# A hybrid two-block layer on one core: experts in pairs on the two column halves of TensorE, in plain full precision, with longer rings for their weights

## The reference

```python
def hier_moe(h, w_group, b_group, w_expert, b_expert, w_gate_e, w_up_e, w_down_e):
    ...
    g_top, g_idx = lax.top_k(g_prob, 1)
    ...
    e_top, e_idx = lax.top_k(e_prob, TOP_K)
    w = g_top * e_top / jnp.sum(e_top, axis=-1, keepdims=True)
    ...
    for e in range(N_EXPERTS):
        a = jax.nn.silu(h @ w_gate_e[e]) * (h @ w_up_e[e])
        y = y + gates[:, e:e + 1] * (a @ w_down_e[e])
    return y
```

## Time and profile before

| what | us |
|---|---|
| median of three runs | 2104.88 |
| fastest run | 2102.53 |
| slowest run | 2868.25 |
| span of the profiled execution | 2102.3 |

### The profile page before, as it was taken

The page is one execution under the profiler, slowest core; times in us unless marked ns, Lnnn a source line. Parts: engine busy times, 40 slices in busy tenths (PEclk is TensorE's granted clock), DMA queues, the critical chain, the costliest instruction groups (busy, mean ns, idle before and its releaser), DMA issues. The chain is left out here.

```text
span 2102.3 us, 25437 instructions
## 1 busy us (share of the span) xinstructions
PE 1936.8 (92%) x8950; PEld 1391.0 (66%) x8954; DVE 1116.4 (53%) x1765; ACT 756.8 (36%) x1230; POOL 234.0 (11%) x285
## 2 busy tenths in 40 slices
PE   4997995799999689999999999998999999999997
PEld 2445644566666356676788887874667678888785
DVE  3787734687878568765222222345976622222235
ACT  2034421355555232672233332222277213333222
POOL 1000000233323134001000000003500100000001
PEclk9999997899999899999999999999999999999998
DMA  9162013599997620022033342331002213335131
GB/s 378 64 240 83 24 58 120 189 362 366 356 353 280 245 81 1 22 91 80 21 100 96 89 154 70 114 119 74 1 22 91 61 32 92 96 100 160 60 100 41
DMA packets 148058, 267.18 MB, mean 127 GB/s; under 512 B 11456, under 2 KB 108736, under 8 KB 134784
## 3 DMA queue, kind: packets, MB, share of 16 engines
q1 hardware_dynamic: 141776, 256.29, 34.5%
q0 software_dynamic: 6192, 9.70, 1.4%
HBM read 257.57 MB, written 20.97 MB: 132 GB/s over the span
## 5 line engine op out<-in xcount | busy, mean ns | idle before, releaser
L274 PE MATMUL bank<-ht_hi,gate_up_hi 128*128 128x512 f32 x704 | 274.2, 389 | 3.4 <-ACT arena L1441 3.4
L276 PE MATMUL bank<-ht_hi,gate_up_lo 128*128 128x512 f32 x704 | 274.0, 389 | 0.0
L275 PE MATMUL bank<-ht_lo,gate_up_hi 128*128 128x512 f32 x704 | 274.0, 389 | 0.0
L2412 PE MATMUL bank<-arena 128*128 128x512 f32 (+3 forms) x640 | 196.4, 466 | 8.0 <-ACT arena L1288 5.5
L1769 DVE TENSOR_TENSOR expert_gate_up_lo<-expert_gate_up,expert_gate_up_hi 128x2048 fp32r<-128x2048 f32 x64 | 146.6, 2292 | 58.0 <-ACT expert_gate_up_hi L1204 58.0
L2066 DVE TENSOR_TENSOR arena<-arena,bank 128x512 f32 (+1 forms) x44 | 30.3, 688 | 272.6 <-ACT arena L1307 272.6
L2412 PEld LDWEIGHTS bank<-arena 128*128 128x128 f32 x640 | 114.7, 196 | 84.4 <-issue 67.0
L274 PEld LDWEIGHTS bank<-ht_hi,gate_up_hi 128*128 128x128 f32 x704 | 132.2, 188 | 31.5 <-issue 4.2
L275 PEld LDWEIGHTS bank<-ht_lo,gate_up_hi 128*128 128x128 f32 x704 | 132.2, 188 | 27.6
L276 PEld LDWEIGHTS bank<-ht_hi,gate_up_lo 128*128 128x128 f32 x704 | 132.2, 188 | 27.3
L1204 ACT CAST expert_gate_up_hi<-expert_gate_up 128x2048 fp32r<-128x2048 f32 x64 | 121.6, 1901 | 72.0 <-PE bank L276 71.9
(11 more groups left out here) (359 smaller groups left out, 3510.2 us busy)
## 6 DMA issues: line engine op xcount, KB each, us to landing
gate_up_whole<-w_gu SPq DMA_DIRECT2D x88, 512.0 KB, 5.0
expert_gate_up<-w_gate_e SPq DMA_DIRECT2D x32, 1024.0 KB, 7.1
expert_gate_up<-w_up_e SPq DMA_DIRECT2D x32, 1024.0 KB, 9.8
arena<-w_down_e SPq DMA_DIRECT2D x32, 1024.0 KB, 5.2
down_whole<-w_down SPq DMA_DIRECT2D x44, 512.0 KB, 3.5
arena<-w_ada SPq DMA_DIRECT2D x5, 4096.0 KB, 20.5
arena<-w_in SPq DMA_DIRECT2D x4, 2048.0 KB, 15.9
w_o_whole<-w_o SPq DMA_DIRECT2D x2, 4096.0 KB, 13.5
```

The costliest lines, as they stand in the source:

```text
L274: pe.matmul(ps, xh, wh, start=start, stop=False)
L275: pe.matmul(ps, xh, wl, start=False, stop=False)
L276: return pe.matmul(ps, xl, wh, start=False, stop=stop)
L2412: ins = pe.matmul(ps[:, 0:b - a], HT[:, c, t * P:(t + 1) * P], w_in2[j][:, c], start=c == 0, stop=c == C8 - 1)
```

## The change

Experts are taken in pairs. The left 64 columns of PE's array hold the first 64 rows of the even expert's window, the right 64 columns those of the odd one. For each of the 8 feature blocks one matmul goes to each half, with that expert's own gate and up weights moving, and both write the same bank, one to partitions 0 to 63, the other to 64 to 127. All is done on the float32 values as they are loaded, with no high and low parts, so ACT and DVE have no splitting. PE's list is no longer staggered: gate and up of a pair, its transposes, its down matmuls, then the next pair. The loops over experts are written out.

Rows beyond an expert's first 64 are taken in windows of 128 after the last pair, one window at a time, in a loop that runs at least once (`extras`). For each such window the expert's three matrices are loaded once more and the whole array is used. DVE works out which expert and which column each of them has.

The ring for gate and up has five slots, the one for down four. Loads: experts 0 and 1 complete, with the router's weights ahead of them, once the attention's output is turned; gate and up of 2 and 3 after the last mixing matmuls, their down tiles after the token rows; gate and up of expert 4 when all sorted rows are in `XsT`. Then in turn, per pair p: when its gate and up matmuls have ended, gate and up of experts 2p+5 and 2p+6; when its down matmuls have ended, down of 2p+4 and 2p+5. The slot lists for storing have 32 columns (16 pairs, up to 16 extra windows) in place of 128. The tiles move within the same arena to make room.

```diff
-        ring_hi = [part(f"expert_gate_up_hi{n}", base + 4 * GU + 2 * DN + n * (GU // 2), 2, C8 // 2, FE) for n in range(2)]
-        stage = [at(base + 3 * GU, T, D), H]
+        ring = [*(at(base + n * GU, 2, C8, FE) for n in range(4)), at(H0 + 2 * D, 2, C8, FE)]
+        ring_d = [at(base + 4 * GU + n * DN, 2, D) for n in range(DN_RING)]
```

SP:

```diff
-            with sp.Fori(1, NE // 4) as it:
-                for s in range(4):
-                    refill(it * 4 + s, it * 4 + s, it * 4 + s - 2, s)
+            load_gate_up(4, gu_slot(4))
+            for p in range(EPAIRS - 2):
+                sp.wait_ge(m_gu, p + 1)
+                for e in (2 * p + 5, 2 * p + 6):
+                    if e < NE:
+                        load_gate_up(e, gu_slot(e))
+                sp.wait_ge(m_y, p + 1)
+                for e in (2 * p + 4, 2 * p + 5):
+                    load_down(e, dn_slot(e))
...
+            with sp.Fori(0, extras) as x:
+                e = sp.value_load(extra_i[0:1, 0, bass.ds(x, 1)], min_val=0, max_val=NE - 1)
+                sp.wait_ge(m_gfree, x + 1)
+                load_gate_up(e, gu_slot(NE))
+                sp.wait_ge(m_dfree, x + 1)
+                load_down(e, dn_slot(NE))
```

ACT:

```diff
-                act.copy(ring_hi[half], ring[s][:, :, 4 * half:4 * half + 4]).then_inc(m_whi, 1)
+            def silu(p, b):
+                act.wait_ge(m_gu, p + 1)
+                act.activation(SG[:, b], bank[b][:, 0:FE], ACT.Silu).then_inc(m_silu, 1)
```

DVE:

```diff
-                dve.tensor_tensor(ring_lo[s][:, :, c4], ring[s][:, :, c4], ring_hi[half].bitcast(F32), ALU.subtract).then_inc(m_wlo, 1)
+            def window(p):
+                for h in range(2):
+                    w0 = dve.value_load(win[0:1, 2 * p + h:2 * p + h + 1], min_val=0, max_val=2 * S)
+                    ins = dve.tensor_copy(XW[p % 2][:, :, HALF * h:HALF * h + HALF], XsT[:, :, bass.ds(w0, HALF)])
+                ins.then_inc(m_xw, 1)
...
+            for p in range(EPAIRS):
...
+                product(p, b)
+                if p + 2 < EPAIRS:
+                    dve.wait_ge(m_gu, p + 1)
+                    window(p + 2)
...
+                copy_ya(p, b)
+            extras = dve.value_load(n_extra[0:1, 0:1], min_val=1, max_val=EXTRAS)
+            with dve.Fori(0, extras) as x:
+                w0 = dve.value_load(extra_i[0:1, 1, bass.ds(x, 1)], min_val=0, max_val=2 * S)
+                dve.wait_ge(m_gu, x + EPAIRS)
+                dve.tensor_copy(XW[0], XsT[:, :, bass.ds(w0, P)]).then_inc(m_xw, 1)
...
```

PE:

```diff
-            with pe.Fori(0, last) as g:
-                for s in range(3):
-                    gate_up(g * 4 + s + 1, g, s + 1)
-                    down(g * 4 + s, g, s)
-                    turn_a(g * 4 + s + 1, s + 1)
+            for p in range(EPAIRS):
...
+                for e in (2 * p, 2 * p + 1):
+                    pe.wait_ge(s_gu[gu_slot(e)], 32 * (e // len(GU_SLOT) + 1))
+                for c in range(C8):
+                    for h in range(2):
+                        ins = pe.matmul(bank[b][half_rows(h)], XW[b][:, c, half_rows(h)], ring[gu_slot(2 * p + h)][:, :, c], start=c == 0, stop=c == C8 - 1)
+                ins.then_inc(m_gu, 1)
...
+                turn_a(p, b)
+                pe.wait_ge(m_atc, p + 1)
...
+                for e in (2 * p, 2 * p + 1):
+                    pe.wait_ge(s_dn[dn_slot(e)], 16 * (e // DN_RING + 1))
+                for half in range(2):
+                    for c in range(2):
+                        for h in range(2):
+                            ins = pe.matmul(bank[4 + 2 * b + half][half_rows(h)], AT[:, b, c, half_rows(h)],
+                                            ring_d[dn_slot(2 * p + h)][:, c, 512 * half:512 * half + 512], start=c == 0, stop=c == 1)
+                ins.then_inc(m_y, 1)
```

More of the change, by code:

```diff
@@ L1239, in _ @@
-            copy_at(0, 0)
-            def step(n, g, s, ahead):
-                g2, s2 = (g, s + 2) if s < 2 else (g + 1, s - 2)
-                if ahead:
-                    gate_up_high(n + 2, g2, s2, 0)
-                silu(n + 1, (s + 1) % 4)
-                if ahead:
-                    gate_up_high(n + 2, g2, s2, 1)
-                copy_y(n, g, s)
-                copy_at(n + 1, (s + 1) % 4)
-            with act.Fori(0, last) as g:
-                for s in range(4):
-                    step(g * 4 + s, g, s, True)
@@ L1257, in weight_second @@
+            with act.Fori(0, extras) as x:
+                act.wait_ge(m_a, x + EPAIRS)
+                silu(x + EPAIRS, 0)
+                act.wait_ge(m_y, x + EPAIRS)
+                copy_at(x + EPAIRS, 0)
+                act.wait_ge(m_st[0], 16 * (EPAIRS // 2 + x))
+                copy_y(x + EPAIRS, 0)
             def weight_second(t):
@@ new lines, in product, with copy_ya @@
+            def product(p, b):
+                dve.wait_ge(m_silu, p + 1)
+                dve.tensor_tensor(A[:, b], SG[:, b], bank[b][:, FE:], ALU.mult).then_inc(m_a, 1)
+            def copy_ya(p, b):
+                dve.wait_ge(m_y, p + 1)
+                dve.tensor_copy(Y[:, b, 0:512], bank[4 + 2 * b][:]).then_inc(m_ya, 1)
+            own.settle()
+            window(0)
+            window(1)
+            for p in range(EPAIRS):
+                b = p % 2
+                if p >= 2:
+                    dve.wait_ge(m_at, p - 1)
+                product(p, b)
+                if p + 2 < EPAIRS:
+                    dve.wait_ge(m_gu, p + 1)
+                    window(p + 2)
+                if p >= 2:
+                    dve.wait_ge(m_st[b], 16 * (p // 2))
+                copy_ya(p, b)
@@ L2382, in _ @@
-            for s in range(3):
-                gate_up(last * 4 + s + 1, last, s + 1)
-                down(last * 4 + s, last, s)
-                turn_a(last * 4 + s + 1, s + 1)
-            down(last * 4 + 3, last, 3)
-            pe.wait_ge(m_y, n_rounds * NE + M_CREDIT)
+                if DN_AT_EXTRA == p:
+                    pe.wait_ge(m_y, p + 1)
+                    pe.sem_inc(m_dfree, 1)
+            pe.wait_ge(s_extra, 1)
+            extras = pe.value_load(n_extra[0:1, 0:1], min_val=1, max_val=EXTRAS)
@@ new lines, in _ @@
+            with pe.Fori(0, extras) as x:
+                sg, sd = gu_slot(NE), dn_slot(NE)
+                pe.wait_ge(m_xw, x + EPAIRS + 1)
+                pe.wait_ge(m_a, x + EPAIRS)
+                pe.wait_ge(s_gu[sg], 32 * (x + GU_USES_EXTRA + 1))
+                for c in range(C8):
+                    ins = pe.matmul(bank[0][:], XW[0][:, c], ring[sg][:, :, c], start=c == 0, stop=c == C8 - 1)
+                ins.then_inc(m_gu, 1)
+                pe.wait_ge(m_gu, x + EPAIRS + 1)
+                pe.sem_inc(m_gfree, 1)
+                pe.wait_ge(m_atc, x + EPAIRS)
+                turn_a(x + EPAIRS, 0)
+                pe.wait_ge(m_atc, x + EPAIRS + 1)
+                pe.wait_ge(m_ya, x + EPAIRS)
+                pe.wait_ge(m_yb, x + EPAIRS)
+                pe.wait_ge(s_dn[sd], 16 * (x + DN_USES_EXTRA + 1))
+                for half in range(2):
+                    for c in range(2):
+                        ins = pe.matmul(bank[4 + half][:], AT[:, 0, c], ring_d[sd][:, c, 512 * half:512 * half + 512], start=c == 0, stop=c == 1)
+                ins.then_inc(m_y, 1)
+                pe.wait_ge(m_y, x + EPAIRS + 1)
+                pe.sem_inc(m_dfree, 1)
```

383 lines of the change are left out of this document (160 added, 223 removed).

## The result

| kernel | median us | fastest to slowest | runs |
|---|---|---|---|
| before | 2104.61 | 2102.53 to 2868.25 | 4 |
| changed | 2055.49 | 2052.77 to 2058.61 | 4 |

The changed kernel takes 0.977 of the time before, 95% interval 0.9755 to 0.9784: 49 us less, against a forecast of 2060 (range 2046 to 2096). The run of 2868.25 was disturbed and isn't in the ratio. The changed kernel's profiled execution took 2054.31, with a span of 2052.5 (before 2102.3).

A forecast was written before the change was run, and what follows sets the result against it. PE bounded the expert stage and the loads, at 415 GB/s, would take over. Start, loads, last pair, extra window and tail put the results' load at 653.1, 44.9 us earlier: span 2057.4, time 2060, range 2046 to 2096.

The forecast's parts named there:

- first rival: Expert stage: loads stay at 359 GB/s instead of speeding up, 33.7 us more, time 2094; chance 0.15.
- fourth rival: Expert pairs: 512-column halves do not run side by side, a pair takes 22.8 us, about 2167; 0.11 together with the third rival.
- the bound of 2: Before the expert stage: removing the splitting taken as 0, at most 2 us less if POOL's gather issue speeds up.
- (a): Pair 0: starts at 395.1, runs cold for 8.6 us and ends at 403.7; only then may SP refill.
- (c): Middle of the stage: remaining loads, 89.9 MB with rows, run without a break at 415 GB/s, 216.7 us, until 621.9.
- (d): End of the loads: expert 31's gate and up land two down tiles earlier, at 616.8.
- (e): Last pair, 15: takes 12.5 us plus 1.7 for a cold start, ending at 631.0.
- (f): Before the loop for rows beyond 64: DVE's serial window preparation, 3.6 us together, until 634.6.
- (h): Tail after the extra window: the present 4.3 us until the results' load, at 653.1.
- (g): Extra window at full width: 12.5 us plus 1.7 cold, until 648.8.
- second rival: Expert stage: PE's clock falls in part of each pair so PE stays the bound; 2078 at clock 0.70; chance 0.16.
- third rival: Expert stage: PE at low clock throughout, 22.9 us a pair, 107 us over the loads, 2167; 0.11 together with the fourth rival.

The follow-up runs named there:

- turns of eight: Changed kernel with all eight matmuls of the left half issued before the right's, down matmuls in turns of two; 2121.43 us (one run).
- waits filled: Changed kernel plus 28 matmuls per pair that nobody reads, placed where PE waits for ACT, DVE and the down tiles; 2057.41 us.
- turns of four: Changed kernel with the two column halves of gate and up issued four matmuls at a time instead of one; 2065.82 us (one run).
- window copied ahead: Changed kernel with DVE copying the extra window's columns before the last pair's product instead of after its result; 2050.61 us.
- gate's bytes only: Changed kernel without loading up weights, gate weights standing in; 2033.14 us, or 2022.92 with small matmuls added in each pair's two waits (one run each).
- window between: Changed kernel with the extra window copied early and its gate and up matmuls between the last pair's transposes and down matmuls; 2049.35 us.

## Why the prediction came out right, step by step

**The bound.** Right: share 1.01 and PE waiting for down tiles. The first rival (359 GB/s) is out: it is 421 to 422 over 150 us, with the scattered rows among it. The Trainium skill's figure of about 358 GB/s per core ("DMA: Bandwidth & Descriptors", section "Specifications") does not hold for this kernel on one core. The same page's section "Bandwidth" says that its larger figure, 425 GB/s for 16 MB, is of a core whose neighbour is idle, and with that the trace's 421 to 422 agree. The forecast had four loads under way and called them 20 us of data; 20 us at 415 GB/s are eight loads, and seven to ten are what the trace shows. The data were right and the count was not.

**PE per pair.** 6.9 and 3.4 were forecast for the two sets; 7.04 and 3.65 are shown, a pair 12.7 instead of 12.5. The fourth rival (no overlap at 512 columns) is out, but the turns of eight and four show that it depends on the order in which the code issues the halves: its 14.06 is the limit for long turns. I had read the overlap from rows 5, whose lines alternate, and hadn't asked whether alternating was what made it. The Trainium skill ("TensorE: Matmul & The Clock Gate", section "The mechanism") says that matmuls start and end in program order; that long turns lose most of the overlap fits it. But in that order strictly only the last matmul of a half could have one of the other half beside it, 0.88 us for each change of half, and 1.71 to 1.82 were saved, about two matmuls. The records don't name their half, so how the second matmul comes in stays open.

**The start.** Forecast 395.1, measured 395.44. That it agrees to 0.3 us is luck: in the ten other profiles of kernels with the changed kernel's routing and sorting the stage starts between 392.97 and 396.25. The parts were called equal on thin ground. Without the splitting, and without the new arithmetic, it starts at 390.35, earlier than in any of them and 4.3 us earlier than before. So the first splits' going gave something, probably more than the bound of 2 that I set, and the new arithmetic with the second window's copy took about as much back; with that scatter, and one profile of each, how much can't be told.

**Steps (a) to (c).** Pair 0 was to be cold, 8.6 us until 403.7; it ran warm, 7.09, and the refill was asked for at 402.56. The down tile of expert 31, issued at 603.0, landed 19.1 us later, at 622.1, against 621.9. That this agrees to 0.2 us is luck: the queue started 1.1 us earlier and in the middle ran at 421 for 415, together some 4 us to the good, and slow ends took them back. Up to 450 the mean is only 401. At the other end the extra expert's gate and up, which SP issues at 605.31, share the queue with the last down tiles, where I had put them wholly behind; but they aren't the cause, since without them the tile lands at the same time, with only 187 GB/s moved from 617 to 622. The last loads come slower than the full queue's rate.

**Steps (d) and (e).** Expert 31's up tile, issued at 592.57, landed 24.5 later, at 617.1, against 616.8. Pair 15 ended at 630.8 (627.12 and 3.65), against 631.0, and this too is luck in its parts. It started only at 617.89, 1.1 us later than forecast, mostly because PE was at the cold down matmuls of pair 14 until 617.48; it took 12.9 us for 12.5; and it ran warm, so the 1.7 that I had charged for a cold start didn't come.

**Steps (f) to (h).** The wait for the window, 2.74 for 3.6. The extra window took 12.9 (633.51 to 646.44) and not 14.2, since it ran warm. The end from there to the results' load is 4.24, against 4.3. The load went out at 650.68, against 653.1. Of the 2.4 us by which my sum was too high at this point, 0.2 had come up by pair 15's end, 0.9 are the wait's in (f) and 1.3 lie in (g), a cold start of 1.7 that didn't come less 0.4 by which the warm window is longer than 12.5. None of the three cold starts that I charged, in (a), (e) and (g), came in this profile. They aren't settled by the program: in (a) the set was cold in the profiles of six of the other kernels, in (g) in four.

**After the stage.** I took it as unchanged; it is 1401.8 us of the span against 1404.3 (spans less 650.68 and 698.04). The same code takes 1398.3 to 1405.7 in the other profiles of this study, so 2.5 us can't be told from its scatter. This, and the 2.4 us above, are the 4.9 us between the forecast span, 2057.4, and 2052.5.

**The clock.** The second rival was half right. The clock does fall, to 0.86 in one window, but only down matmuls are cold; gate and up take 7.04 to 7.09 in all 16 pairs. The Trainium skill, "TensorE: Matmul & The Clock Gate", section "HAM oscillation", tells of a loop in which every burst starts cold. The forecast took this stage for such a loop, and it isn't quite one: in the page's loop the wait for DMA is longer than the work between two waits, and here the longest wait inside a pair is 2.44 us while every set takes 3.65 or more. The trace has eight down sets cold and no gate and up set. With rings of 4 and 4, where the gate and up matmuls wait for their up tile, it is the other way round: four sets of gate and up in the middle are cold, 8.76 to 8.78 us, after waits of 2.65 to 3.21, and only one of down. The low clock was hidden, as I had charged it: with the waits filled nothing was won. But the cover is thin: a cold down takes a pair from 12.7 to 14.4, against the loads' 15.7. With turns of four a pair is 14.5 warm and 16.2 cold, and that was enough to make PE the bound and lose 10 us. The third rival, low clock throughout, appeared nowhere. The argument that I had against it was too strong, though: rows 7 themselves have PE busy without a gap from 404 to 408 at 0.61.

## What to carry to other kernels

When PE stops being the bound, work out what the loads cost at the rate of a window in which the queue is full, not at the stage's mean: here 415 GB/s gave the landing of the last tile to a fraction of a microsecond, with some luck, where the stage's own 334 would have been wrong by a quarter. Lay out the rings so that the queue is never short of work, and don't forget the tile that is released last: going from two down tiles to four was worth some 23 us here, the fifth gate and up tile about 4, if anything. Where two column halves are to run side by side, issue them in turns of one or two matmuls, and look at what the last, unpaired piece costs: one expert in 32 took 13.5 us, as much as a pair.

## What the hardware showed that was not expected

- Column halves overlap only near a change of half: 16 gate and up matmuls take 7.04 us in turns of one, 8.92 in turns of four, 12.24 in turns of eight; 8 down matmuls take 3.65 in turns of one and 3.71 in turns of two.
- The first burst's clock is not set by the wait ahead of it alone. In nine kernels with the same order of matmuls PE was idle for 3.71 to 3.77 us ahead of pair 0, each time until DVE's window copy. Its 32 records took 7.09 us in four of them (the changed kernel, the window copied ahead, the two with gate's bytes only) and 8.78 in five (both shorter rings, the window between, no extra window, filled waits). Why isn't settled.
- At the same waits of 1.16 and 0.52 us the down matmuls are cold in some pairs and warm in others: 6 of 16 sets with gate's bytes only, 8 of 16 with turns of four. With the waits cut to 0.18 us none is.
- The DMA share can stay at 1.00 while the rate falls from 421 to 404 GB/s. With mostly two to five loads of 1 MB under way (rings of 4 and 2) it was 404; with mostly four to seven (turns of four) and with seven to eleven (the changed kernel) 421.
- The last loads of a queue come slower than its rate: without the extra window's loads 246 GB/s from 615 to 620, where 423 had moved from 605 to 610.
